# The V pass of a PEER layer with the table tiles stationary, and the closing norm of its gathered token tile moved inside that pass

## What is computed

```python
s1, i1 = lax.top_k(s[:, :, 0], PEER_TOPK)
s2, i2 = lax.top_k(s[:, :, 1], PEER_TOPK)
...
gate = jax.nn.softmax(top, axis=-1)
act = jax.nn.gelu(jnp.einsum('td,thkd->thk', hb, u_tab[eidx]).astype(jnp.float32), approximate=False)
wts = (gate * act).astype(hb.dtype)
return jnp.einsum('thk,thkd->td', wts, v_tab[eidx])
...
f = _peer(h2.reshape(b * t, d), w_peer_q, peer_subkeys, peer_u, peer_v).reshape(b, t, d)
x = x + gt2 * _rmsnorm(f, g_post_ffn)
```

## Time and profile before

| what | value |
|---|---|
| median of 3 runs | 2131.84 us (2126.91 to 2135.81) |
| profiled execution, its own time | 2130.17 us |
| its span in the trace | 2128.4 us |
| TensorE / VectorE / ScalarE / GpSimd busy | 94% / 46% / 7% / 20% |
| DMA, mean over the span | 369 GB/s |
| U pass, first to last matmul (L1025) | 829 to 1462 us |
| V pass (L1039, L1042) | 1462.7 to 2095.3 us |
| from the last V matmul to the span's end | 33.1 us |

### The profile page before, as it was taken

How to read it: one execution, slowest core, us unless ns; L and a number is a source line. 1 busy time by engine, 2 the same in 40 slices (tenths; PEclk the granted TensorE clock), 3 DMA queues, 4 the chain that set the end, 5 groups by cost and what they waited for, 6 DMA issues and landing times.

```text
span 2128.4 us, 26880 instructions
## 1 busy us (share of the span) xinstructions
PE 2000.5 (94%) x11303; PEld 1327.2 (62%) x11303; DVE 982.4 (46%) x1650; ACT 150.5 (7%) x346; POOL 425.0 (20%) x391
## 2 busy tenths in 40 slices
PE   5799999999999999999999999999999999999996
PEld 0255777766664778989998999996333333333333
DVE  0300030111004579668989389975444444444422
ACT  1100001211001200000010110000000000000001
POOL 0001443351000124222423111102111111111100
PEclk7899999999999999999999999999999999999998
DMA  9989987699668799999999989979999999999982
GB/s 388 422 331 400 369 333 287 228 359 358 249 232 322 288 393 409 421 421 420 420 417 421 415 344 410 402 279 413 422 421 421 421 421 421 421 421 421 421 311 75
DMA packets 123120, 784.88 MB, mean 369 GB/s; under 512 B 15408, under 2 KB 19632, under 8 KB 36480
## 3 DMA queue, kind: packets, MB, share of 16 engines
q1 hardware_dynamic: 67568, 447.37, 52.2%
q0 software_dynamic: 55440, 335.86, 39.0%
HBM read 777.90 MB, written 5.28 MB: 368 GB/s over the span
## 4 chain that ended last, share of the span: by engine, by line
PE 63%; DMA 33%; DVE 2%; issue 1%; POOL 1%; ACT 1%; SPq 0%; DVEq 0%; POOLq 0%
DMA ring<-peer_v 19%; PE PS L1025 17%; PE PS L698 17%; DMA ring<-u_tiles 10%; PE PS L1039 8%; PE PS L901 6%; DMA ring<-w_ada 3%; PE PS L627 3%; PE PS L1042 2%; PE PS L1003 2%; PE PS L718 1%; PE PS L839 1%; POOL ring L382 1%; DMA ring<-cache_k,pg_i 1%; PE PS L948 1%
## 5 line engine op out<-in xcount | busy, mean ns | idle before, releaser
L1025 PE MATMUL PS<-hT,ring 128*128 128x160 f32 x4096 | 575.5, 300 | 18.0 <-DMA ring<-u_tiles 17.6
L1025 PEld LDWEIGHTS PS<-hT,ring 128*128 128x128 f32 x4096 | 559.0, 190 | 28.6 <-issue 28.6
L1039 PE MATMUL PS<-ring,big 128*128 128x512 f32 x1024 | 473.6, 605 | 33.3 <-DMA ring<-peer_v 32.6
L1427 DVE SCALAR_TENSOR_TENSOR big<-ring,big 128x2048 f32<-128x2048 f32 x128 | 300.9, 2351 | 306.3 <-DMA ring<-peer_v,uidx 306.1
L1039 PEld LDWEIGHTS PS<-ring,big 128*128 128x128 f32 x1024 | 184.0, 189 | 331.2 <-issue 199.0
L698 PE MATMUL PS<-hT,ring 128*128 128x288 f32 x1536 | 380.8, 408 | 1.8 <-DMA ring<-w_in 1.7
L698 PEld LDWEIGHTS PS<-hT,ring 128*128 128x128 f32 x1536 | 289.2, 190 | 88.6 <-issue 11.6
L1416 DVE SCALAR_TENSOR_TENSOR ring<-ring,big 128x2048 f32<-128x2048 f32 x128 | 291.2, 2289 | 97.0 <-DMA ring<-peer_u,uidx 95.0
L395 POOL DMA_INDIRECT ring<-peer_u,uidx x128 | 176.3, 1378 | 690.0 <-DVE ring L1416 445.8
L395 POOL DMA_INDIRECT ring<-peer_v,uidx x128 | 122.2, 955 | 545.7 <-DVE big L1427 522.6
L1042 PE MATMUL PS<-ring,big 128*32 128x512 f32 x1024 | 136.4, 605 | 0.0
(11 more groups left out here) (259 smaller groups left out, 985.2 us busy)
## 6 DMA issues: line engine op xcount, KB each, us to landing
ring<-u_tiles SPq DMA_DIRECT2D x128, 1024.0 KB, 12.2
ring<-peer_v SPq DMA_DIRECT2D x128, 1024.0 KB, 14.9
ring<-w_ada SPq DMA_DIRECT2D x96, 1024.0 KB, 12.2
ring<-w_in SPq DMA_DIRECT2D x32, 1024.0 KB, 8.7
ring<-w_out SPq DMA_DIRECT2D x16, 1024.0 KB, 5.0
ring<-w_pq SPq DMA_DIRECT2D x16, 1024.0 KB, 9.3
xT<-x_t SPq DMA_DIRECT2D x1, 2304.0 KB, 27.0
kv_out<-big SPq DMA_DIRECT2D x1, 2304.0 KB, 12.3
```

The lines of the kernel that those rows point to most:

```text
L1025: last = mm(PS[:, bank, 0:ND], ring[:, r, P * k:P * (k + 1)], hT[:, k, P:NT], start=(k == 0), stop=(k == KC - 1))
L1039: mm(PS[:, j, :], W[:, n, 0:P], ring[:, r, 512 * j:512 * (j + 1)], start=(n == 0), stop=(n == KEYS - 1), skip_group_check=True)
L1427: v.scalar_tensor_tensor(h2n, ring[:, r, :], act[:, n:n + 1], h2n, ALU.mult, ALU.add).then_inc(used[r], 1)
```

## The change

**The V pass.** Each 1 MB tile of `peer_v` is now the stationary operand, in 16 pieces of 128 x 128, and `W[:, n, :]` with all 160 tokens moves past it, so there are 16 matmuls with 160 columns where there were 8 with 512. The sums stand in PSUM by feature and token: feature chunk k (128 features x 160 tokens) in bank k // 3, three chunks to a bank, banks 0 to 5. The gate matmuls of the U pass use banks 6 and 7 in place of 5 and 6.

**The gathered tile.** Its squares, root and diagonal matrix (`spread0`) are computed as soon as `f_ready` stands, while the V pass runs. Its turn is put inside the V pass: 8 matmuls after V tile 122 and 8 after V tile 125 (`TURN_AT`), into banks 6 and 7; VectorE adds each half to `xT`, and tile 0's part of `y_out` is written first.

**The closing norm of the 160 dense tokens** is done by feature: ScalarE squares the 16 chunks (`fsq`), TensorE sums them over features with 16 matmuls of a matrix of ones, VectorE meanwhile multiplies the chunks with the gain (`gain_chunks`), then come the root, the reciprocal, and for each half of the features a multiplication and an addition to `xT`, each half written out by itself.

```diff
+    TURN_AT = (KEYS - 6, KEYS - 3)
...
-        for t, (c0, c1) in enumerate((TILE_COLS[1], TILE_COLS[2], TILE_COLS[0])):
+        for t, (k0, k1, c0, c1) in enumerate(((0, KC, 0, P), (0, 8, P, NT), (8, KC, P, NT))):
             sp.wait_ge(y_ready, t + 1)
-            sp.dma_start(y_out[:, :, c0:c1], xT[:, :, c0:c1]).then_inc(out_done, 16)
+            sp.dma_start(y_out[:, k0:k1, c0:c1], xT[:, k0:k1, c0:c1]).then_inc(out_done, 16)
...
+        r, i = dense_slot(V0 + 31)
+        a.wait_ge(used[r], PEER.used0 + i + 1)
+        a.wait_ge(f_ready, 1)
+        fn(big[:, 0:D], h2n, ACT.Square, accum_out=fss).then_inc(sums_ready, 1)
+        a.wait_ge(fvar_ready, 1)
+        fn(fss, fss, ACT.Sqrt).then_inc(froot_ready, 1)
...
+        for part, (k0, k1) in enumerate(F_CHUNKS):
+            if part:
+                a.wait_ge(fg_ready, 1)
...
+            last.then_inc(fsq_ready, 1)
+        root(3, P, NT)
...
-                last = mm(PS[:, 5 + g % 2, P * q:P * (q + 1)], hits2[g % 2][:, q, :], hits1[g % 2][:, q, :],
+                last = mm(PS[:, 6 + g % 2, P * q:P * (q + 1)], hits2[g % 2][:, q, :], hits1[g % 2][:, q, :],
...
-            for j in range(4):
-                mm(PS[:, j, :], W[:, n, 0:P], ring[:, r, 512 * j:512 * (j + 1)],
-                   start=(n == 0), stop=(n == KEYS - 1), skip_group_check=True)
-            for j in range(4):
-                last = mm(PS[32 * j:32 * j + 32, 4, :], W[:, n, P:ND], ring[:, r, 512 * j:512 * (j + 1)],
-                          start=(n == 0), stop=(n == KEYS - 1), skip_group_check=True)
+            for k in range(KC):
+                last = mm(PS[:, k // 3, ND * (k % 3):ND * (k % 3 + 1)], ring[:, r, P * k:P * (k + 1)], W[:, n, :],
+                          start=(n == 0 and k % 3 == 0), stop=(n == KEYS - 1), skip_group_check=True)
             last.then_inc(used[r], 1)
...
+            if n in TURN_AT:
+                part = TURN_AT.index(n)
+                if part:
+                    pe.wait_ge(half_kept, 1)
+                else:
+                    pe.wait_ge(spread_ready, 1)
+                for k in range(8):
+                    last = mm(PS[:, 6 + k // 4, P * (k % 4):P * (k % 4) + P],
+                              h2n[:, P * (8 * part + k):P * (8 * part + k + 1)], spread0, start=True, stop=True)
+                last.then_inc(fT_done, 1)
...
+        for part, (k0, k1) in enumerate(F_CHUNKS):
+            pe.wait_ge(fsq_ready, part + 1)
+            if not part:
+                pe.wait_ge(half_kept, 2)
+            for k in range(k0, k1):
+                last = mm(PS[:, 7, 0:ND], ones, fsq[:, k, :], start=(k == 0), stop=(k == KC - 1))
+        last.then_inc(ssq_done, 1)
...
+        dve.wait_ge(fg_ready, 1)
+        norm(3, P, NT, 7)
+        for k0 in (0, 8):
+            part = fg[:, k0:k0 + 8, :]
+            own(v.tensor_tensor(part, part, rstd[:, P:NT].unsqueeze(1).broadcast_to([P, 8, ND]), ALU.mult))
+            v.tensor_tensor(xT[:, k0:k0 + 8, P:NT], xT[:, k0:k0 + 8, P:NT], part, ALU.add).then_inc(y_ready, 1)
```

More of the change, by code:

```diff
@@ L210, in build @@
     grec = mxs[:, 8:16]
-    fss = mxs[:, 16:19]
+    fss = mxs[:, 16:17]
     iota = cst[:, C_IOTA:C_IOTA + P]
@@ L215, in build @@
     hits1 = [hT[:, 8 + 4 * n:12 + 4 * n, 0:P] for n in range(2)]
-    spreads = [hT[:, n, P:2 * P] for n in range(3)]
-    fT = hT
+    spread0 = hT[:, 0, 0:P]
+    F_CHUNKS = ((0, 9), (9, KC))
+    fsq, fg = hT[:, :, P:NT], big[:, 0:KC * ND].rearrange("p (k t) -> p k t", t=ND)
     def sem(name):
@@ L593, in _ @@
                 fn(fresh[:, n % 4, :], PS[:, n % 3, 0:ND], ACT.Gelu).then_inc(emptied[n % 3], 1)
+        r, i = dense_slot(V0 + 31)
[4 more added lines that the diff above has]
+        fn(fss, fss, ACT.Sqrt).then_inc(froot_ready, 1)
         r, i = dense_slot(V0 + KEYS - 1)
         a.wait_ge(used[r], PEER.used0 + i + 1)
[L597 to L600, removed]
-        a.wait_ge(fvar_ready, 1)
-        fn(fss, fss, ACT.Sqrt).then_inc(froot_ready, 1)
-        a.wait_ge(sample_done, 1)
-        fn(fT[:, :, NP_TOK:NT].rearrange("p (j c) m -> p j c m", c=4),
-           PS[:, 6, :].rearrange("p (c j m) -> p j c m", c=4, j=4), ACT.Copy).then_inc(fT_kept, 1)
+        for part, (k0, k1) in enumerate(F_CHUNKS):
+            if part:
+                a.wait_ge(fg_ready, 1)
+            for b in (range(k0 // 3, k1 // 3 + 1) if part else ()):
+                n = min(3, KC - 3 * b)
+                last = fn(fsq[:, 3 * b:3 * b + n, :], PS[:, b, 0:n * ND].rearrange("p (c t) -> p c t", c=n), ACT.Square)
+            if not part:
+                last = fn(fsq[:, k0:k1, :].rearrange("p (b c) t -> p b c t", c=3),
+                          PS[:, 0:3, 0:3 * ND].rearrange("p b (c t) -> p b c t", c=3), ACT.Square)
+            last.then_inc(fsq_ready, 1)
+        root(3, P, NT)
     @blk.tensor
@@ L1545, in _ @@
         own(v.reciprocal(fss, fss))
[L1546 to L1553, removed]
-            return last
@@ L1556, in _ @@
[L1556 to L1566, removed]
@@ L1567, in _ @@
-        add_tile(0, 0, KC).then_inc(y_ready, 1)
+        v.tensor_scalar(spread0, ident, fss, None, ALU.mult).then_inc(spread_ready, 1)
+        for part in range(2):
+            dve.wait_ge(fT_done, part + 1)
+            for n in range(8):
+                k = 8 * part + n
+                last = v.scalar_tensor_tensor(xT[:, k, 0:P], PS[:, 6 + n // 4, P * (n % 4):P * (n % 4) + P],
+                                              G2[:, k, 0:1], xT[:, k, 0:P], ALU.mult, ALU.add)
+            last.then_inc(half_kept, 1)
@@ new lines, in _, with gain_chunks @@
+        dve.wait_ge(half_kept, 2)
+        dve.sem_inc(y_ready, 1)
+        def gain_chunks(k0, k1):
+            b, n = k0 // 3, k1 - k0
+            f = PS[:, b:b + n // 3, 0:3 * ND].rearrange("p b (c t) -> p b c t", c=3)
+            to = fg[:, k0:k1, :].rearrange("p (b c) t -> p b c t", c=3)
+            g = G2[:, k0:k1, :].rearrange("p (b c) n -> p b c n", c=3)
+            v.tensor_tensor(to[:, :, :, 0:P], f[:, :, :, 0:P], g[:, :, :, 0:1].broadcast_to([P, n // 3, 3, P]), ALU.mult)
+            for j in range(n // 3):
+                new = f[:, j, :, P:ND].rearrange("p c (b i) -> p c b i", i=NQ)
+                last = v.tensor_tensor(to[:, j, :, P:ND].rearrange("p c (b i) -> p c b i", i=NQ), new,
+                                       g[:, j, :, 1:NROW].unsqueeze(3).broadcast_to([P, 3, NB, NQ]), ALU.mult)
+            return last
@@ new lines, in _ @@
+        r, i = dense_slot(V0 + KEYS - 1)
+        dve.wait_ge(used[r], PEER.used0 + i + 1)
+        gain_chunks(9, 15)
+        v.tensor_scalar(fg[:, 15, 0:P], PS[:, 5, 0:P], G2[:, 15, 0:1], None, ALU.mult)
+        v.tensor_tensor(fg[:, 15, P:ND].rearrange("p (b i) -> p b i", i=NQ),
+                        PS[:, 5, P:ND].rearrange("p (b i) -> p b i", i=NQ),
+                        G2[:, 15, 1:NROW].unsqueeze(2).broadcast_to([P, NB, NQ]), ALU.mult).then_inc(fg_ready, 1)
+        dve.wait_ge(fsq_ready, 1)
```

24 lines of the change are left out of this document (8 added, 16 removed).

## The result

The changed kernel took 2120.76 us (median of 12 runs, 2117.12 to 2128.94) beside 2132.87 us for the kernel before (12 runs): a ratio of 0.9949, interval 0.9931 to 0.9967, so 0.5% faster, some 11 us. The ratio goes by the means of the fast runs, without one run of the kernel before that took 3448.18 us. The forecast was 2117 us within 2111 to 2124, and faster. The profiled execution took 2122.56 us, its span 2120.8 us.

A forecast was written before the change was run, and what follows sets the result against it. Transfers were taken to bound the U and V passes, TensorE only the end. The tail's 14.9 us less and the last tiles' +0.5 made 14.4 us, from a median of 2131.84 to 2117 us, range 2111 to 2124.

The forecast's parts named there:

- The tail: From ScalarE's start after the last V tile to the end: 18.1 us against 33.0, 14.9 us less.
- sums: In the tail, the closing sums with ones on TensorE: 32 passes of 160 columns, 4.35 us at full clock.
- a wide operation: In the tail, each of VectorE's two multiplications and two additions of 1280 elements: 1.48 us each, 5.9 us in all.
- from the last addition to the end: In the tail, the last write of the output: 4.2 us, far bound 5.55.
- The last tiles: The last 11 V tiles, TensorE the bound: 3.1 us gained, 3.6 us paid for the two turns, net +0.5 us.
- the full-clock price: Price of the turns' 32 passes amid dense work: 0.111 us each, 3.6 us; the other price, far bound, 5.5 us.
- low clock in the sums: Rival in the tail: TensorE's clock falls, the 32 passes of the sums double, +4.35 us, 2122 us; chance 0.12.
- late gathers: Rival: the last gathered row lands as late as 2069, so the turn waits 6 us, 2123 us; chance 0.05.
- faster V pass: Rival: a round of V tiles shrinks by 0.28 us, 7.6 us more gain, 2110 us; chance 0.06.
- loads in series: Rival: TensorE's weight loads are not overlapped, a V tile takes 6.1 us, 2269 us; chance 0.03.
- a fixed landing: Premise of the faster V pass rival: a landing takes 14.95 us however much is in flight; chance 0.06.
- I cost it at nothing: V pass up to tile 117: a tile's 4.35 us in place of 4.63 is hidden under landings of 4.98 us.

The follow-up runs named there:

- late turns: The changed kernel with both turns of the gathered tile moved back behind the last V tile: 2126.89 us, ratio 0.9984.
- double square: The changed kernel with ScalarE's first squares of the tail made twice, so TensorE idles longer before the closing sums: 2122.76 us in a single run.
- two more matmuls: The changed kernel with two more matmuls, their result unused, in each of V tiles 0 to 111: 2120.51 us, ratio 0.9954.
- bfloat16 sums: The changed kernel with the closing norm's squares in bfloat16, summed in one pass for each chunk in place of two: 2121.43 us, ratio 0.994.
- the two with the old form: The kernel before, 2132.87 us, and the kernel before with only the gathered tile's squares, root and turns put under the V pass, 2127.7 us.

## Why the prediction was right, and where not

- **The tail: right.** 18.0 us measured, 18.1 forecast. Terms: squares 1.37 (1.37), sums 4.61 (4.35), mean, root and reciprocal 0.33 + 0.34 + 1.15 = 1.82 (1.8), a wide operation 1.49 (1.48), from the last addition to the end 3.9 (4.2). That the sum is met to 0.1 us is a little luck: the sums are 0.3 us over, the end 0.3 under.
- **The last tiles: right.** t117 to V1 took 51.7 us for 50.9, +0.7 where +0.5 stood. A turn costs 1.78 us (1.8), and none waits: the full-clock price was the right one of the two.
- **The rivals did not occur.** No low clock in the sums (1.00), no late gathers (the last sum ends 2.2 us after t117, as before), no faster V pass (421 GB/s again), no loads in series (26.35 us for six tiles). That more TensorE work left the time alone speaks against a fixed landing too.
- **Wrong: "I cost it at nothing" for the V pass up to tile 117.** It was taken from one round of 19.90 us in the U pass. A loss that comes once in several rounds, as the one below does, can't be seen in one. The five profiles with the new form whose transfers were left alone (changed, late turns, double square, two more matmuls, bfloat16 sums) took 584.0, 584.1, 582.3, 583.4 and 583.4 us, mean 583.4; the two with the old form 581.7 and 581.1. So +2.0 us, where the five lie within 1.8 us of each other, and the change is worth 14.4 - 2.0 = 12.4; the medians differ by 12.1.

Where the 2 us sit can be read from the gathered rows. Nearly all start 4.97 us after the one before, with 2.6 us of idle time on VectorE; a few come late. Those over 1.2 us late in the kernel before, then all those of the changed one, then the four latest of the kernel with two more matmuls (0.8 to 0.95 us; five of 0.3 to 0.6 us are left out):

```profile
1535.58 2.35 DVE L1427 SCALAR_TENSOR_TENSOR big<-ring,big 128x2048 f32<-128x2048 f32 x1 [4.32 <-DMA ring<-peer_v,uidx]
1855.31 2.35 DVE L1427 SCALAR_TENSOR_TENSOR big<-ring,big 128x2048 f32<-128x2048 f32 x1 [4.32 <-DMA ring<-peer_v,uidx]
```
```profile
1485.02 2.35 DVE L1437 SCALAR_TENSOR_TENSOR big<-ring,big 128x2048 f32<-128x2048 f32 x1 [3.92 <-DMA ring<-peer_v,uidx]
1645.42 2.35 DVE L1437 SCALAR_TENSOR_TENSOR big<-ring,big 128x2048 f32<-128x2048 f32 x1 [4.18 <-DMA ring<-peer_v,uidx]
1805.93 2.35 DVE L1437 SCALAR_TENSOR_TENSOR big<-ring,big 128x2048 f32<-128x2048 f32 x1 [4.09 <-DMA ring<-peer_v,uidx]
1966.49 2.35 DVE L1437 SCALAR_TENSOR_TENSOR big<-ring,big 128x2048 f32<-128x2048 f32 x1 [4.16 <-DMA ring<-peer_v,uidx]
```
```profile
1483.87 2.35 DVE L1440 SCALAR_TENSOR_TENSOR big<-ring,big 128x2048 f32<-128x2048 f32 x1 [3.40 <-DMA ring<-peer_v,uidx]
1624.46 2.35 DVE L1440 SCALAR_TENSOR_TENSOR big<-ring,big 128x2048 f32<-128x2048 f32 x1 [3.55 <-DMA ring<-peer_v,uidx]
1765.12 2.35 DVE L1440 SCALAR_TENSOR_TENSOR big<-ring,big 128x2048 f32<-128x2048 f32 x1 [3.57 <-DMA ring<-peer_v,uidx]
1910.79 2.35 DVE L1440 SCALAR_TENSOR_TENSOR big<-ring,big 128x2048 f32<-128x2048 f32 x1 [3.48 <-DMA ring<-peer_v,uidx]
```

Against 2.61 us, the two before lose 2 x 1.71 = 3.4 us; the four after lose 1.31 + 1.57 + 1.48 + 1.55 = 5.9: 2.5 us more, beside the 2.3 measured. They come at a fixed distance: 320 us before, 160 after, 141 to 146 with two more matmuls. In tiles of 4.97 us that is 64, 32 and 28 to 29. A tile has 32 matmuls and weight loads on TensorE before (16 passes), 64 after and 72 with the two more, and 64 x 32 = 32 x 64 = 2048, with 72 x 28.4 as well. So every 2048 TensorE instructions the transfers slip by some 1.5 us (with two more matmuls about the same is lost in smaller pieces). The Trainium skill, "Runtime: NRT & Kernel Launch", Instruction fetch mechanics, says that TensorE's instruction memory holds 2048 instructions and is refilled by a DMA queue, and that the refill is mostly hidden. The distance agrees. TensorE does not wait for its code: of its 45.5 us of idle time in the V pass 45.1 end with a landing of `peer_v`. But the transfers that it waits for do slip.

The start of every packet in the trace ties the slips to the loads. Queue q8 brings 16 KB at a time, some 40 us apart in the V pass before and 20 after, so about 256 of TensorE's instructions each. Each late row shown, and the packet that started before it:

| | row | packet of q8 | between |
|---|---|---|---|
| before | 1535.58, 1855.31 | 1533.40, 1853.14 | 2.2 us |
| changed | 1485.02, 1645.42, 1805.93, 1966.49 | 1482.85, 1642.79, 1803.29, 1963.87 | 2.2 to 2.6 us |
| two more matmuls | 1483.87, 1624.46, 1765.12, 1910.79 | 1477.81, 1618.40, 1759.68, 1904.74 | 5.4 to 6.1 us |

From one of these packets to the next it is the eighth each time, and eight times 256 is 2048. In the first two kernels no row behind the seven between is over 0.25 us late.

Shown, then: that the loss is no TensorE time, that it comes by TensorE's instruction count, 2.2 to 6.1 us after a load of its code has started, and that loading code costs transfers on another queue. Argued only: that the load is the cause of the slip, since no run changed TensorE's code alone. Why one load in eight costs 1.3 to 1.7 us and the seven between nothing, and why q14's smaller packets cost 0.5 to 0.8 us each, stays open.

The median lies 4 us above the forecast: 2 us are this, and 1 us is the base, since the kernel before had 2132.87 us in twelve runs where the forecast started from 2131.84 in three. The rest is less than the spread of the runs.

## What to carry to other kernels

Where transfers fill the DMA, an edit that leaves bytes and buffers alone can still cost them: count the instructions that it adds, on engines that are idle too, and look at the instruction queues of the page. A tail in which engines take turns is priced well by adding the durations of like rows, and what another engine can do under the last loop is best put there, with the handovers left under tiles. And ask which of two streams is to end first: when the one that no one needs at the end stops early, the other is left with its consumer as the bound.

## What was not expected of the hardware

- Straight-line increments of a semaphore that nothing waits for made a stretch of 582 us 34 to 39 us longer, through the loading of 0.36 MB of code on VectorE or 0.66 MB on the idle ScalarE; on ScalarE in a loop they cost next to nothing (583.9 us beside 583.4).
- A gap of 2.70 us on TensorE kept the full clock, while two of 2.25 and 2.34 us with 2 us of work between them were followed by 0.73.
